# The first block of a two-block network written as one scheduled stage instead of eleven

## The reference

```
h    = rmsnorm(x, norm_g)                      # 512 x 1024
proj = h @ w_in                                # q_lat 384, kv_lat 256, k_pe 32, conv b/c/u 512 each,
                                               # q_mem 512, gates 3 x 512, r 3 x 1024
q    = rmsnorm(q_lat) @ w_uq                   # 8 heads x 96
kv   = rmsnorm(kv_lat) @ w_ukv                 # 8 heads x (64 key + 64 value)
q, k = rope(rmsnorm per head(q)), rope(rmsnorm per head([k_nope, k_pe]))
o_attn = softmax(q k^T / sqrt(96)) v * silu(g_attn)            # 8 heads, 512 x 512 scores
o_conv = c_b * conv3(c_c * c_u) * silu(g_conv)                 # depthwise, 3 taps
mkv  = rmsnorm(mem) @ w_mkv                                    # 256 tokens, 4 heads x (128 + 128)
o_mem  = softmax(rmsnorm(q_mem) rmsnorm(m_k)^T / sqrt(128)) m_v * silu(g_mem)
y    = sum over the three branches of sigmoid(r + b) * (o @ w_br)
x    = x + y @ w_out
```

## Time and profile before

| | |
|---|---|
| median of three runs | 2214.79 us |
| profiled execution, time | 2212.33 us |
| profiled execution, span | 2210.5 us |
| PE busy, whole span | 2081.3 us (94%) |
| first block, from its first weight product to the first one with `w_out` (37.36 to 727.29) | 689.93 us |
| stages 3 (132 to 189.5) | 57.5 us, clock 0.63 |
| stage 4 (189.5 to 270) | 80.5 us |
| stages 5 to 8 (270 to 385.6) | 115.6 us, clock 0.85 |
| stage 9, 10, 11 | 90.4, 47.9 and 203.4 us |
| second block (790 to the end) | 1420 us, PE busy 1383.36 us |

### The profile page before, as it was taken

The page is one execution under the profiler, slowest core; times in us unless marked ns, Lnnn a source line. Parts: engine busy times, 40 slices in busy tenths (PEclk is TensorE's granted clock), DMA queues, the critical chain, the costliest instruction groups (busy, mean ns, idle before and its releaser), DMA issues. The chain is left out here.

```text
span 2210.5 us, 24162 instructions
## 1 busy us (share of the span) xinstructions
PE 2081.3 (94%) x9497; PEld 1624.5 (73%) x9497; DVE 768.2 (35%) x1402; ACT 757.5 (34%) x1196; POOL 755.3 (34%) x327
## 2 busy tenths in 40 slices
PE   6887987999999889999989999999999988999998
PEld 5633483877888776666678888887888877888887
DVE  4147414233111235555332222225557523222222
ACT  4343444223333244445333322322222223332231
POOL 2131040444666322221234444433223133444442
PEclk7877997999999999999999999999999989999999
DMA  4110030432333221111123333322222112333331
GB/s 127 48 29 0 26 100 9 105 82 71 100 100 103 83 64 48 48 48 30 58 67 96 95 102 99 95 77 77 58 67 59 48 58 67 96 98 102 95 96 58
DMA packets 267410, 159.56 MB, mean 72 GB/s; under 512 B 6073, under 2 KB 265249, under 8 KB 267298
## 3 DMA queue, kind: packets, MB, share of 16 engines
q1 hardware_dynamic: 267298, 158.02, 24.7%
HBM read 155.91 MB, written 2.10 MB: 71 GB/s over the span
## 5 line engine op out<-in xcount | busy, mean ns | idle before, releaser
L227 POOL TENSOR_TENSOR weight_lo<-weight_stage,weight_hi 128x1024 fp32r<-128x1024 f32 x303 | 734.1, 2429 | 1378.4 <-ACT weight_hi L217 1054.2
L217 ACT ACTIVATE weight_hi<-weight_stage 128x1024 fp32r<-128x1024 f32 x303 | 318.9, 1054 | 417.4 <-PE bank L244 417.4
L244 PE MATMUL bank<-a_hi,weight_lo 128*128 128x512 f32 x1040 | 412.3, 396 | 24.6 <-DVE a_lo L346 9.7
L244 PE MATMUL bank<-a_lo,weight_hi 128*128 128x512 f32 x1040 | 409.2, 393 | 0.0
L244 PE MATMUL bank<-a_hi,weight_hi 128*128 128x512 f32 x1040 | 409.0, 393 | 0.0
L244 PEld LDWEIGHTS bank<-a_hi,weight_lo 128*128 128x128 f32 x1040 | 197.5, 190 | 73.3 <-issue 20.8
L244 PEld LDWEIGHTS bank<-a_hi,weight_hi 128*128 128x128 f32 x1040 | 197.7, 190 | 42.3
L244 PEld LDWEIGHTS bank<-a_lo,weight_hi 128*128 128x128 f32 x1040 | 197.9, 190 | 39.9
L244 PE MATMUL bank<-hidden_hi,weight_lo 128*128 128x512 f32 x512 | 199.5, 390 | 0.0
L244 PE MATMUL bank<-hidden_hi,weight_hi 128*128 128x512 f32 x512 | 199.3, 389 | 0.0
L244 PE MATMUL bank<-hidden_lo,weight_hi 128*128 128x512 f32 x512 | 199.3, 389 | 0.0
(11 more groups left out here) (284 smaller groups left out, 2929.7 us busy)
## 6 DMA issues: line engine op xcount, KB each, us to landing
weight_stage<-in_mlp_w SPq DMA_DIRECT2D x128, 512.0 KB, 3.9
weight_stage<-in_w_in SPq DMA_DIRECT2D x57, 512.0 KB, 3.8
weight_stage<-in_hg_w_in SPq DMA_DIRECT2D x32, 512.0 KB, 4.0
weight_stage<-in_sb_w_qkv SPq DMA_DIRECT2D x24, 512.0 KB, 3.7
weight_stage<-in_w_mkv SPq DMA_DIRECT2D x8, 512.0 KB, 4.2
weight_stage<-in_w_out SPq DMA_DIRECT2D x8, 512.0 KB, 3.9
weight_stage<-in_sb_w_o SPq DMA_DIRECT2D x8, 512.0 KB, 3.8
weight_stage<-in_hg_w_o SPq DMA_DIRECT2D x8, 512.0 KB, 4.0
```

Of the source, the lines that this page charges most:

```text
L217: act.activation(self.hi[slot][:, :], self.stage[slot][:, :], ACT.Copy).then_inc(self.hi_done, 1)
L227: pool.tensor_tensor(self.lo[slot][:, :], self.stage[slot][:, :], self.hi[slot][:, :].bitcast(F32), ALU.subtract).then_inc(self.split_done, 1)
L244: last = pe.matmul(out, l, r, start=n == 0, stop=n == 3 * len(pairs) - 1)
```

## The change

The eleven blocks become one (`first_block`, new). What changes in it:

- **Order of work on PE.** Latent projections (key/value latents first), then the four memory queries with the transposing of `mem` between their products, then key/value heads, query heads, memory keys and values. Then sixteen rounds ("doubles": two heads, 128 queries), in each of which 24 convolution products are placed around the transposes, scores, value products and spreads of the attention. Then sixteen memory items with the products of the gates between them, then the mix.
- **Column norms.** Sums of squares of heads are put in a column per head and 128 tokens (as `ModelNorm` does), and DVE takes the reciprocal root by ten small instructions on columns (`newton`, in use in the second block already). For queries the factor is never multiplied in: it goes into the exponential as `scale`, and into the bias by a product of one column (`crest`). Keys are still multiplied, by a spread factor.
- **Silu from tanh.** ACT computes tanh(g/2), and DVE (t + 1) * g, and then 0.5 * that * o. Exp and tanh are in one table; the order of ACT after the change has two table loads behind the sines up to the end of the mix, where before there were seven.
- **y is split inside the mix**, so `add_to_x` gets `hi` and `lo` ready.
- **Convolution in two banks** (0 and 1) that alternate, and so each unit waits for a use of the one before the last.
- Storage is shared by many names; the 128 x 896 constants of the HGRN2 masks are no longer loaded at the start (the constants shrink from 1288 to 392 columns) but by a DMA at the start of the HGRN2 stage.

The diff, cut to its core (new code of `first_block`, PE's side first):

```diff
-        add("latent", 5, 1, lambda f, r: win(f))
+        add("latent", 5, 1, lambda f, r: win((3, 4, 0, 1, 2)[f]))
...
+        add("qmem", 4, 1, lambda f, r: qmem(f))
+        add("ukv", 2, 1, ...)
         add("uq", 3, 1, ...)
-        add("ukv", 2, 1, ...)
-        add("qmem", 4, 1, lambda f, r: qmem(f))
...
-            sp.dma_start(S.const[:, :], consts).then_inc(loaded, 16)
+            sp.dma_start(S.const[:, :], consts[:, 0:K_LEVEL]).then_inc(loaded, 16)
...
+    def root(self, dve, sums, width):
+        dve.tensor_scalar(self.mean, sums, 1.0 / width, EPS, ALU.mult, ALU.add).then_inc(self.steps, 1)
+        dve.wait_ge(self.steps, 1)
+        newton(dve, self.steps, 1, self.mean, self.rstd, self.half)
...
+                for n in range(2 * HEADS):
+                    head(n)
+                    if n == 0:
+                        sums(("mq", 3), S.ps[7], 3 * NT)
+                    if n == 1:
+                        mem_cols.ready(pe)
+                        mem_cols.spread(pe, S.ps[6], 0, NM).then_inc(mem_spread, 1)
+                    if 2 <= n < 2 + HEADS:
+                        key_sums(n - 2)
+                    if n >= 2 + HEADS:
+                        query_sums(n - 2 - HEADS)
+                    if n in (12, 14):
+                        turn_v(n // 2 - 6)
+                for n in range(2 * MEM_HEADS):
+                    whole(mem_kv(n))
...
+                for m in range(DOUBLES):
+                    p, i = divmod(m, NT)
+                    fill(conv, 2 if m == 0 else 4)
+                    if m >= 1:
+                        turn(m - 1)
+                    if m + 1 < DOUBLES:
+                        score(m + 1)
+                    fill(conv, 4)
+                    if p + 1 < PAIRS:
+                        if i < 2:
+                            key_spread(2 * p + 2 + i)
+                        elif i == 2 and p + 2 < PAIRS:
+                            turn_v(p + 2)
...
+                    if m >= 1:
+                        weigh(m - 1)
+                gate = gates()
...
+                for n in range(ITEMS):
+                    fill(gate, 2)
+                    mem_turn(n)
+                    if n + 2 < ITEMS:
+                        mem_score(n + 2)
+                    fill(gate, 2)
+                    if n >= 1:
+                        mem_weigh(n - 1)
...
+                def crest(n, bank, keys, cols, c):
+                    dve.wait_ge(scored, n + 1)
+                    dve.tensor_reduce(peak[:, n:n + 1], bank[:, 0:keys], AX.X, ALU.max, negate=True).then_inc(peaked, 1)
+                    dve.wait_ge(peaked, n + 1)
+                    dve.tensor_tensor(bias[:, n:n + 1], peak[:, n:n + 1], cols.rstd[:, c:c + 1],
+                                      ALU.mult).then_inc(biased, 1)
...
+                def silu(tile, bank, free):
+                    dve.scalar_tensor_tensor(out=tile, in0=tile, scalar=1.0, in1=bank, op0=ALU.add,
+                                             op1=ALU.mult).then_inc(free, 1)
...
+                        for r in range(2):
+                            keep(item(m - 1, r), S.ps[4 + r], T)
+                        conv_unit(m - 1)
...
-    return add_to_x(S, W.first["out"], S.ahi, S.alo, norm2, split=S.scratch)
+        return add_to_x(S, W.first["out"], y_hi, y_lo, norm2)
...
+                sp.dma_start(levels[:, :], S.consts[:, K_LEVEL:K_COLS]).then_inc(levels_loaded, 16)
```

More of the change, by code:

```diff
@@ new lines, with __init__, ready, spread @@
+class Columns:
+    def __init__(self, S, columns, name, n):
+        self.S, self.n = S, n
+        self.mean, self.rstd, self.half = columns(n), columns(n), columns(n)
+        self.steps = S.sem(f"{name}_newton")
+    def root(self, dve, sums, width):
+        dve.tensor_scalar(self.mean, sums, 1.0 / width, EPS, ALU.mult, ALU.add).then_inc(self.steps, 1)
+        dve.wait_ge(self.steps, 1)
+        newton(dve, self.steps, 1, self.mean, self.rstd, self.half)
+    def ready(self, eng):
+        eng.wait_ge(self.steps, NEWTON + 1)
+    def spread(self, pe, bank, first, count, rows=P):
+        for i in range(count):
+            last = pe.matmul(bank[0:rows, i * P:(i + 1) * P], self.rstd[:, first + i:first + i + 1].to_broadcast([P, rows]),
+                             self.S.eye, start=True, stop=True)
+        return last
@@ L1243, in mix_branches, with item @@
+        u_mkv, u_conv, u_gate, u_mix = f["mkv"], f["conv"], f["gates"], f["mix"]
+        END = u_mix + 48
+        kg = VEC["k_head_g"]
+        k_gain = S.vec[:, kg:kg + 1]
+        def item(m, r):
+            return 2 * m + r
         with nc.Block() as block:
@@ new lines, in sums @@
+                def sums(key, bank, first, rows=slice(0, P), tokens=NT, start=None, stop=None):
+                    pe.wait_ge(squared, SQ[key] + 1)
+                    sq = square_of(key)
+                    for i in range(tokens):
+                        last = pe.matmul(bank[:, first + i:first + i + 1], sq[rows, i * P:(i + 1) * P], S.ones[rows, 0:1],
+                                         start=True if start is None else start and i == 0,
+                                         stop=True if stop is None else stop, skip_group_check=start is not None)
+                    last.then_inc(summed, 1)
@@ new lines, in _, with fill @@
+                for n in range(2 * MEM_HEADS):
+                    whole(mem_kv(n))
+                    if n < 2:
+                        query_sums(HEADS - 2 + n)
+                        key_spread(n)
+                    elif n % 2 == 0:
+                        mem_key_sums(n // 2 - 1)
+                conv = convolution()
+                def fill(steps, n):
+                    for _ in range(n):
+                        next(steps, None)
+                score(0)
+                fill(conv, 2)
```

1434 lines of the change are left out of this document (757 added, 677 removed).

## The result

The changed kernel took 2114.11 us (median of four runs, 2110.09 to 2116.89) against 2214.6 in the same session: 0.9545 of the time, 95% interval 0.9529 to 0.9562. The profiled execution has a span of 2111.1 us, where that of before had 2210.5. The predicted 2117 is 3 us off, but errors of the working cancel in it, and a claim beside it was wrong.

What follows compares the result with a forecast made beforehand. PE bounds the kernel; its first-block work of 576.8 us plus 11.8 waits and 8 hand-offs gives 597 against 689.93. 2212.33 - 93 - 4 - 1 = 2114, with the median 2.5 above: 2117, range 2097 to 2155.

Steps and rivals of the forecast that it cites:

- rival C: Before the first scores: heads remain a chain and PE waits at a join; 2128; chance 0.76 together with forecast and D.
- A: In the doubles: DVE comes late with POOL's holds and PE waits up to one per unit; 2135 to 2166; chance 0.19.
- B: In the doubles: PE waits for DVE, its clock falls to 1.2 GHz and the kernel ends slower; chance 0.03.
- Value products: In PE's summed work: 160 pieces of 128 columns at 0.21 us each, 33.6 us (32 to 36).
- A double: In the attention: PE's work of one double, with 24 products, scores, transposes, value products, mostly a spread or transposes: 10.8 us.
- Hand-offs of 8: In the attention: POOL's holds of DVE hidden in most doubles; 8 us allowed in all (0 to 57).
- 4, the same size as the 4.1 now: Before the query heads: PE waits for weights, 4.7 us less 0.8 of sums beside it, 4 us.
- The join of 3.3: End of the mix: last product by a gate, sum, rounding and rest in sequence, with the barrier: 3.3 instead of 4.80 us.
- the predicted 4: First two w_out units: ready operands make 14.9 us into 10.9, 4 less (0 if the clock falls in the gap).
- The second block "isn't touched": Second block: dense and not touched by the change, so it should be as long as before.
- The start: -1: Start: 448 KB of constants aren't loaded; 1 us less, 1.7 at most, 0 if the vectors land later anyway.
- "The gain doesn't lie in laying products beside the attention, which PE alone bounds already": First block: PE already bounds the attention, so the gain lies in the norms and joins; 93 us less in the stretch.

Runs made afterwards that it cites:

- the run with the two parts: Changed kernel with the first four query heads' products by weight tiles 0 and 1 ahead of those by tile 2: 2106.62 us, ratio 0.9505.
- the second profile: The changed kernel run and profiled once more, with no edit: 2115.15 us, ratio 0.955.
- the 64 bytes: Changed kernel with 64 unused bytes a partition ahead of the storage that the stages share: 2100.32 us, ratio 0.9483.

## Why the prediction was right, and what in it was wrong

- **The main claim held.** PE's work with few waits sets the first block: 582.8 us, of which 11.8 idle, against 597 predicted. The clock is at the high level from the end of the first unit to the mix but for one place, no wait stands before the first scores (195.05, rival C is out), and the doubles never wait (A and B are out).
- **Value products, sized wrongly.** The step "Value products ... I take 0.21". From the start of eight to the next product, they take 1.02 us, 0.128 each, since two heads' pieces of 64 outputs run in pairs. I had priced them from pieces of full width or of one head. 128 of them in the doubles: 10.5 us too much.
- **A double** is (346.41 - 208.22)/14 = 9.87 us by the starts of its transposes, not 10.8. One with neither spread nor transposes of values or keys takes 9.31 where the working has 10.0, and the value products explain that. The 0.8 for "mostly a spread or transposes" stood in every double: with a spread it is 10.18, with such transposes 9.8 to 9.95, and four of sixteen have neither. That second error is only in the room of a double; the sum counts spreads and transposes one by one.
- **Hand-offs of 8:** 3.0 us, all in the memory items, where the prediction saw the smaller room. POOL does hold DVE, 12 of its 48 peak products by up to 2.2 us, and in the doubles the room hides every hold: PE was full for 170 of 170 us.
- **"4, the same size as the 4.1 now"** for the weights of the query heads: 3.7. What the step left out is the clock behind it, 4.8 us more in this profile and 2.6 in the second, as the run with the two parts shows. The wait of 4.1 before had cost another 2.4 in the same way; the step took the wait from the earlier trace rows without looking at the products behind it. This omission and the hand-offs that were priced too high cancel: with the slow first unit, all waits and slow products come to 11.8 + 3.0 + 4.8 = 19.6, where 11.8 + 8 were allowed. PE's own work is what came out less, 563 for 576.8; beside the 10.5 of the value products, and against 3.5 lost in the mix, some 6 us of that (an estimate from these figures) were not traced to a term.
- **The join of 3.3** was 3.17. The first two `w_out` units took 11.28 instead of 14.9: 3.6 of the predicted 4. That was luck: in the second profile the clock fell in this gap, they took 14.07, and the 4 were nearly the 0 that the working names for that case. The slow first unit is as said: 39.22 to 53.05 for two.
- **The second block "isn't touched".** It lost 9.4 us beside `w_out`'s gain, and the mix too went at 0.230 a product instead of 0.226 (864 in 199 us; with the 64 bytes 0.227). I took "none of these changes in number" for "none changes in price". The storage's move was in the change, and its cost was bounded by nothing in the working.
- **The start: -1 was +1.9.** The constants' part is right, PE began at 9.14 instead of 10.39. But in both profiles with the old first block three setup tiles ran at the high clock, 1.28 us apart; in the ten with the new one and without unused products none did. With such counts it is hardly chance, the time of the start isn't it either, and the cause stays open.
- **"The gain doesn't lie in laying products beside the attention, which PE alone bounds already"** is wrong as a statement on the changed kernel. The 107 us hold some 34 that only the threading gives. It was argued from an attention without the keys' work in it; once that work moved inside, DVE and ACT set the bare double. The total came out all the same, because the sum counted PE's work and checked the room.

So the mechanism of the first block is right, but that the time is only 3 us off is luck: 14 too little gain in the stretch, and 13 of losses (9.8 in the rest, 2.9 at the start) that weren't foreseen, cancel.

## What to carry to other kernels

Add up the bounding engine's work and check the room of each hand-off; but price small matmuls from the very pattern they will have, and look at the products behind a wait too: those of 3.7 to 4.1 us here were followed by products at 1.2 GHz that cost another 2 to 5. After every edit that changes storage, compare start-to-start times of products that it didn't touch: a tile that moved by 64 bytes can cost 3% of each. "PE is 96% busy here" speaks of the work that is there now, not of what will be moved in.

## What the runs showed of the hardware

- A matmul of 512 fp32r columns takes 0.227, 0.229 or 0.233 us at full clock by the distance, by 256 bytes, of its moving operand to the tiles laid down first, the weight tiles among them. For the 1536 hidden products, which the change didn't touch, that is about 10 us.
- f32 matmuls with 64 outputs in different halves of a bank's partitions run in pairs: eight in 1.02 us instead of 1.51.
- DVE's hold behind POOL moves: it fell on a product of one column with two inputs in SBUF (2.20 us for 0.16), and when that was made a tensor_scalar, which was never held (48 of 48 in 0.22 us), on the scaling behind it (1.77 for 0.49).
- A wait of PE can bring the clock down or not: behind the same gap of 3.17 us two `w_out` units took 11.28 us in one execution and 14.07 in another.
- Products whose result is thrown away kept the clock up in the setup: 7 us of them before the input had landed, and seven more products in later gaps, brought the first weight product 5 us forward. Of the median they took 3 to 4 us, within overlapping intervals.
